# Attention of a hybrid diffusion block: high and low part of a head's queries stacked in the 128 rows, and values of two units at one visit

## What is computed

```python
def attend_with_sink(q, k, v, sink, mask):
    s = jnp.einsum("bqhgd,bkhd->bhgqk", q, k, preferred_element_type=jnp.float32) * (HEAD_DIM ** -0.5)
    if mask is not None:
        s = jnp.where(mask, s, NEG_INF)
    sk = sink.astype(jnp.float32)[None, :, :, None, None]
    m = jnp.maximum(jnp.max(s, axis=-1, keepdims=True), sk)
    p = jnp.exp(s - m)
    denom = jnp.sum(p, axis=-1, keepdims=True) + jnp.exp(sk - m)
    return jnp.einsum("bhgqk,bkhd->bqhgd", (p / denom).astype(v.dtype), v)
```

## Time and profile before

| | |
|---|---|
| three runs | 1251.46, 1252.09, 1252.34 us (median 1252.09) |
| the profiled execution | 1252.31 us, of which the span of instructions is 1250.5 us |
| TensorE busy | 1241.1 us (99%) |
| VectorE, ScalarE, GpSimd busy | 913.3, 560.5, 340.7 us (73%, 45%, 27%) |
| granted TensorE clock | 0.999 over the span |
| mean DMA rate | 160 GB/s |

### The profile page before, as it was taken

The page is one execution under the profiler, slowest core; times in us unless marked ns, Lnnn a source line. Parts: engine busy times, 40 slices in busy tenths (PEclk is TensorE's granted clock), DMA queues, the critical chain, the costliest instruction groups (busy, mean ns, idle before and its releaser), DMA issues.

```text
span 1250.5 us, 19713 instructions
## 1 busy us (share of the span) xinstructions
PE 1241.1 (99%) x7504; PEld 1074.4 (86%) x7504; DVE 913.3 (73%) x1229; ACT 560.5 (45%) x912; POOL 340.7 (27%) x270
## 2 busy tenths in 40 slices
PE   8999999999999999999999999999999999999998
PEld 6788777787888898888888888899999999998996
DVE  4799889562898777662879674577897566778677
ACT  5223465653423345332223332344676645754554
POOL 1006699110143001111001110003693130144243
PEclk9999999999999999999999999999999999999999
DMA  9666422112466416562555664335433554556553
GB/s 380 221 214 197 147 65 71 65 54 99 143 191 227 136 61 203 186 225 80 182 166 188 212 194 145 122 119 189 150 123 118 175 178 138 186 185 207 180 170 116
DMA packets 52804, 200.33 MB, mean 160 GB/s; under 512 B 6001, under 2 KB 7921, under 8 KB 51569
## 3 DMA queue, kind: packets, MB, share of 16 engines
q1 hardware_dynamic: 52576, 199.13, 48.5%
q10 hardware_dynamic: 144, 0.07, 0.0%
HBM read 196.81 MB, written 1.05 MB: 158 GB/s over the span
## 4 chain that ended last, share of the span: by engine, by line
PE 97%; DVE 1%; ACT 0%; DMA 0%; issue 0%; DVEq 0%
PE psA L640 25%; PE psA L642 25%; PE psA L641 25%; PE psB L642 3%; PE psB L640 3%; PE psB L641 3%; PE psB L993 2%; PE psB L981 2%; PE psB L1140 2%; PE psB L1141 2%; PE psB L1142 2%; PE psA L968 1%; PE psA L646 1%; PE psA L651 1%; PE psA L647 1%; PE psB L675 1%
## 5 line engine op out<-in xcount | busy, mean ns | idle before, releaser
L640 PE MATMUL psA<-h_hi,w_hi 128*128 128x512 f32 (+1 forms) x1448 | 491.5, 339 | 0.1
L642 PE MATMUL psA<-h_hi,w_lo 128*128 128x512 f32 (+1 forms) x1448 | 488.0, 337 | 0.0
L641 PE MATMUL psA<-h_lo,w_hi 128*128 128x512 f32 (+1 forms) x1448 | 487.9, 337 | 0.0
L1196 ACT ACTIVATE w_hi<-raw 128x1024 fp32r<-128x1024 f32 (+2 forms) x246 | 274.2, 1117 | 278.0 <-PE psA L642 166.8
L1565 DVE TENSOR_TENSOR w_lo<-raw,w_hi 128x1024 fp32r<-128x1024 f32 (+2 forms) x246 | 339.4, 1380 | 61.5 <-ACT w_hi L1196 61.0
L640 PEld LDWEIGHTS psA<-h_hi,w_hi 128*128 128x128 f32 x1448 | 274.8, 190 | 29.9 <-DVE w_lo L1565 0.9
L642 PEld LDWEIGHTS psA<-h_hi,w_lo 128*128 128x128 f32 x1448 | 274.8, 190 | 29.1
L641 PEld LDWEIGHTS psA<-h_lo,w_hi 128*128 128x128 f32 x1448 | 274.9, 190 | 28.5 <-issue 0.2
L627 POOL TENSOR_TENSOR hid_lo<-sig,hid_hi 128x512 f32 (+3 forms) x44 | 68.6, 1558 | 441.5 <-ACT hid_hi L1513 441.5
L1597 DVE SCALAR_TENSOR_TENSOR ada_sum<-raw,csil,ada_sum 128x1024 f32<-128x1024 f32 x112 | 156.7, 1430 | 0.0
L2058 DVE SCALAR_TENSOR_TENSOR tmp<-psA,vec,tmp 128x510 f32<-128x510 f32 (+1 forms) x44 | 27.1, 615 | 68.3 <-ACT tmp L1524 68.1
(11 more groups left out here) (246 smaller groups left out, 1814.2 us busy)
## 6 DMA issues: line engine op xcount, KB each, us to landing
raw<-w_up SPq DMA_DIRECT2D x88, 512.0 KB, 4.3
raw<-w_ada SPq DMA_DIRECT2D x80, 512.0 KB, 3.5
raw<-w_in SPq DMA_DIRECT2D x35, 512.0 KB, 4.3
raw<-w_at SPq DMA_DIRECT2D x24, 512.0 KB, 3.5
raw<-w_dn SPq DMA_DIRECT2D x16, 704.0 KB, 5.2
raw<-w_dn SPq DMA_DIRECT2D x22, 512.0 KB, 3.5
raw<-w_fn SPq DMA_DIRECT2D x16, 640.0 KB, 4.1
raw<-w_sc SPq DMA_DIRECT2D x16, 640.0 KB, 3.9
```

The costliest lines, as they stand in the source:

```text
L640: pe.matmul(out, w0, hi, start=first, stop=False)
L641: pe.matmul(out, w0, lo, start=False, stop=False)
L642: return pe.matmul(out, w1, hi, start=False, stop=last)
L1196: act.activation(w_hi[:, s, 0:tiles * P], raw[:, r, 0:tiles * P], ACT.Copy).then_inc(head_done, 1)
```

## The change

Scores. The split queries of a head now lie above each other: `q_two[:, b, half, :]` holds for one head the high part in the 64 partitions of its own half and the low part in the other 64. `k_two[half]` holds the high part of that half's keys twice, in both sets of 64 partitions. One matmul over 128 rows then gives high times high plus low times high. The product with `k_lo` remains a 64-row matmul for each half. The mask band comes after the stacked matmuls.

ScalarE therefore makes four copies of 64 by 512 keys instead of one of 128 by 512, and two copies of 64 by 128 queries per unit instead of one of 128 by 128. VectorE makes the low keys and the low queries in two instructions each; the low queries are written into the partitions of the other half. ScalarE's key copies wait for one more semaphore (`evac`, an event of the stage before), since `k_two[1]` lies in memory that the stage before used.

Values. `values` does nothing for even units and does two units at an odd one: the transposed weights of two units stand side by side (in the first layer in unused ends of the weight slots, `prob_tails`; in the second in unused columns of `h_hi` and `h_lo`, `prob_pair`), and one matmul takes 256 columns. In the first layer the first two key blocks belong to the latent unit alone and stay at 128 columns. `y_hi` and `y_lo` are made for two units at once.

```diff
-        q_hi = place("q_hi", [2, P], F32R)
-        q_lo = place("q_lo", [2, P], F32R)
+        q_two = place("q_two", [2, 2, P], F32R)
...
-        k_hi = at("k_hi", [NT], F32R, sqa_off)
+        k_two = [at("k_two0", [NT], F32R, sqa_off), at("k_two1", [NT], F32R, t_off + 4 * NT * 2)]
...
-                    pe.wait_ge(q_rest, b0 + k + 1)
+                    pe.wait_ge(q_rest, 2 * (b0 + k + 1))
                     b = (b0 + k) % 2
+                    for half in range(2):
+                        pe.matmul(score_bank(layer, half)[:, 0:nk * P], q_two[:, b, half, :],
+                                  k_two[half][:, k0 * P:(k0 + nk) * P], start=True, stop=False, skip_group_check=True)
                     if s == 0:
                         for half in range(2):
                             pe.matmul(score_bank(layer, half)[:, (1 - qi) * P:(2 - qi) * P], band[:, 2, :],
-                                      band[:, qi, :], start=True, stop=False, skip_group_check=True)
-                    for part, (qs, ks) in enumerate(((q_hi, k_hi), (q_hi, k_lo), (q_lo, k_hi))):
-                        for half in range(2):
-                            rows = slice(64 * half, 64 * half + 64)
-                            mm = pe.matmul(score_bank(layer, half)[:, 0:nk * P], qs[rows, b, :],
-                                           ks[rows, k0 * P:(k0 + nk) * P], start=(s == 1 and part == 0),
-                                           stop=(part == 2), skip_group_check=(s == 0))
...
+                                      band[:, qi, :], start=False, stop=False, skip_group_check=True)
+                    for half in range(2):
+                        rows = slice(64 * half, 64 * half + 64)
+                        pe.matmul(score_bank(layer, half)[:, 0:nk * P], q_two[rows, b, half, :],
+                                  k_lo[rows, k0 * P:(k0 + nk) * P], start=False, stop=True, skip_group_check=True)\
+                            .then_inc(s_mm, 1)
...
                 def values(k):
-                    s, qi, t = un[k]
-                    k0, nk = (0, 4) if s == 0 else (2, 2)
+
+                    if k % 2 == 0:
+                        return
                     pe.wait_ge(pt, 2 * (b0 + k) + 2)
-                    if b0 + k:
-                        pe.wait_ge(o_rest, b0 + k)
-                    for b in range(nk):
+                    if b0 + k > 1:
+                        pe.wait_ge(o_rest, b0 + k - 1)
+                    for b in range(4):
+                        n = P if layer == 0 and b < 2 else 2 * P
...
+                            mm = pe.matmul(out_bank[64 * half:64 * half + 64, 0:n],
+                                           v[:, b, 64 * half:64 * half + 64],
+                                           prob, start=(b == 0), stop=(b == 3),
+                                           skip_group_check=True)
+                    mm.then_inc(o_mm, 2)
...
-                    act.activation(q_hi[:, (b0 + k) % 2, :], q[:, t, q0:q0 + P], ACT.Copy).then_inc(q_head, 1)
+                    for half in range(2):
+                        rows = slice(64 * half, 64 * half + 64)
+                        act.activation(q_two[rows, (b0 + k) % 2, half, :], q[rows, t, q0:q0 + P], ACT.Copy).then_inc(q_head, 1)
 
                 act.wait_ge(rope, 15 * (layer + 1))
-                act.activation(k_hi[:, :], k_all[:, :], ACT.Copy).then_inc(k_head, 1)
+                act.wait_ge(evac, n0 + 16)
+                for half in range(2):
+                    for into in range(2):
+                        act.activation(k_two[half][64 * into:64 * into + 64, :], k_all[64 * half:64 * half + 64, :], ACT.Copy)\
+                            .then_inc(k_head, 1)
...
+                    for half in range(2):
+                        rows, others = slice(64 * half, 64 * half + 64), slice(64 - 64 * half, 128 - 64 * half)
+                        dve.tensor_tensor(q_two[others, (b0 + k) % 2, half, :], q[rows, t, q0:q0 + P],
+                                          q_two[rows, (b0 + k) % 2, half, :].bitcast(F32), ALU.subtract).then_inc(q_rest, 1)
+
+                dve.wait_ge(k_head, 4 * (layer + 1))
+                for half in range(2):
+                    rows = slice(64 * half, 64 * half + 64)
+                    dve.tensor_tensor(k_lo[rows, :], k_all[rows, :], k_two[half][rows, :].bitcast(F32), ALU.subtract)\
+                        .then_inc(k_rest, 1)
```

More of the change, by code:

```diff
@@ L440, in wide, with two_units @@
             return (4 if batches(layer)[k][0] == 0 else 2) * P
+        def two_units(layer, y, unit):
+            _, qi, t = unit
+            if layer:
+                return y[:, 3 + t:5 + t, P * qi:P * qi + P]
+            return y[:, 4 + t, :].rearrange("p (s n) -> p s n", s=2)[:, :, P * qi:P * qi + P]
         block = ctx.enter_context(nc.Block())
@@ L952, in scores @@
                     if k == 0:
-                        pe.wait_ge(k_rest, layer + 1)
+                        pe.wait_ge(k_rest, 2 * (layer + 1))
                         pe.wait_ge(v_done, layer + 1)
@@ L1854, in query_rest @@
                     q0 = SEQ * s + P * qi
[L1855 to L1860 removed]
+                    dve.wait_ge(q_head, 2 * (b0 + k + 1))
+                    for half in range(2):
[7 more added lines that the diff above has]
+                        .then_inc(k_rest, 1)
                 for k in range(2):
```

52 lines of the change are left out of this document (27 added, 25 removed).

## The result

| | before | after |
|---|---|---|
| median | 1252.21 us (1251.46 to 1253.94, 6 runs) | 1260.03 us (1259.02 to 1261.73, 6 runs) |
| profiled execution, span | 1252.31, 1250.5 us | 1259.02, 1257.2 us |

The ratio is 1.0063, 95% interval 1.0052 to 1.0073: slower, by 7.8 us. The forecast was 1253.0, range 1250.2 to 1255.8.

The account below looks back on a forecast made before the run. TensorE's streaming plus mode switches was taken to bound the kernel, any new TensorE wait adding in full. Terms -1.7 + 1.9 + 0.2 + 0.3 + 0.2 = +0.9 us gave a median of 1253.0, range 1250.2 to 1255.8.

Parts of the forecast that it names:

- Scores, 0: TensorE's score matmuls: three times 0.23 us per unit before and after, mode switches alike; 0, bounds -2.4 to +2.4 us.
- Values, -1.7: TensorE's values: same columns, but 24 visits become 12, each saving 0.14 us; -1.7 us, bounds 0 to -2.5.
- Transposes earlier, +0.2 and +0.3: Second layer, places 4 and 12: TensorE reaches odd units' transposes earlier and waits for ScalarE's shares; +0.2 and +0.3 us.
- Start of the second layer, +1.9: Second layer's attention start: TensorE's first scores wait for four key copies, then VectorE's low keys and low queries; +1.9 us.
- fifth rival: Behind 884 us: a 2 to 3 us wait drops TensorE's clock to 1.2 GHz, costing about 3 more; 1256 us, chance 0.04.
- Low queries in the first layer, +0.2: VectorE, first layer: the second low-query subtraction follows the first without waiting for GpSimd, costing 0.2; +0.2 us, bounds 0 to 5.
- second rival: VectorE's second subtractions each lose the shared port lock to GpSimd, 0.5 to 1.0 us: 1255.4 to 1258 us, chance 0.25.

Follow-up runs that it names:

- old_helpers: Kernel after's stacked score matmuls, but one key copy, one query copy and one subtraction each as before, values as before; output differs: 1252.94 us against 1252.39.
- values_only: Kernel before with only the values part of the change (two units per visit), six score matmuls and old helpers kept: 1251.41 us against 1252.34.
- small_taps_after: Kernel after with GpSimd's taps 1 to 30 working on 2 columns per stream instead of 256: 1253.40 us, ratio 1.0003 to before.
- three_pairs: The change's scores part alone with all its helper work, but TensorE takes scores as three half-row pairs; output differs: 1261.19 us, ratio 1.0066.
- all_in_two: Kernel before with ScalarE's key and query copies, low-query and low-key subtractions all in pieces of 64 partitions: +7.9 us, ratio 1.0060.
- again_low: Kernel before with an unread 64-partition, 64-column subtraction from partition 0 behind each low-query subtraction, no added signal: 1252.39 us against 1252.35.

## Why the prediction was wrong

**Scores, 0: right.** old_helpers is +0.3 us in the first layer and 0.0 at the second start, within 0.2%.

**Values, -1.7 (0.14 a visit): right.** The first layer of values_only is -1.2 for 8 visits, 0.14 each. In the second layer, from 888.5 to 975 us, it loses 0.5 with a wait of 1.27 in it, so about 0.8 is saved for four visits.

**Transposes earlier, +0.2 and +0.3: wrong in size, and without effect.** In values_only it is 0 at place 4 and 1.27 at place 12, outside my bound of 0.8. In the kernel after there is no wait at either place; I take it that this is because TensorE comes 4.6 us later there.

**Start of the second layer, +1.9: too small; measured 4.6.** I had 1.3 us of wait without GpSimd and 1.9 with it; measured are 2.06 and 2.87. Of the 0.7 that is missing without GpSimd, 0.4 are the copies, whose distance for 64 partitions is 0.65 and not the 0.52 that I took, and 0.3 the subtractions, which start 0.72, 0.72 and 0.32 apart in small_taps_after where I had 0.63, 0.63 and 0.20. The lock adds 0.8. The other 1.7 us come behind the wait: in the table of differences the kernel after loses 3.1 us up to the first branch matmul and 1.5 over the next 3.6 us, where the clock is at 1.2 GHz for the most part. That was my fifth rival, with 0.04; I had its price as 3.

**Low queries in the first layer, +0.2: the step that failed.** It says that the second subtraction follows the first, by the row at 194.03. That row is one of 128 partitions from partition 0, like the one ahead of it; it says nothing of the new ones, which alternate between partitions 0 and 64 and each signal. VectorE and GpSimd in the kernel after, against the earlier trace rows:

```profile
177.11 1.95 DVE L1887 TENSOR_TENSOR q_two<-q,q_two 64x128 fp32r<-64x128 f32 x2
178.98 1.27 DVE L1918 TENSOR_REDUCE small<-psA 128x1 f32<-128x512 f32 x2
...
176.84 1.28 POOL L598 TENSOR_TENSOR acc<-acc,sqb 128x512 f32<-128x512 f32 x1
178.22 0.70 POOL L596 TENSOR_SCALAR sqb<-glu,vec 128x512 f32<-128x512 f32 x1
```

The first waits for the end of L598 (178.12) and the second for that of L596 (178.92); in the earlier trace rows one took 1.29 in all. The term was 0.2 and 4.6 + 1.2 = 5.8 was lost there; 5 was my bound. TensorE's waits in that layer add up to 4.8 (0.4, 1.44, 0.36, 1.09 and 1.45); the trace has no wait for the other 1.0. The second rival had the mechanism and for "1.0 per unit" a first layer of 4 to 5 and 1258 us: that is what happened, with the clock on top. The Trainium skill's rule in "SBUF — State Buffer", section "SBUF: two separate sides", which I cited against the change, is borne out: the second one of a pair lasts 0.53 to 1.36 us in 23 of the 24 pairs of the kernel after and 0.29 in one. I gave that rival 0.25 because one row seemed to speak against it.

**Open.** three_pairs loses 1.1 us more in the first layer than all_in_two. The difference between them in VectorE is that the low queries go to the partitions of the other half, and ScalarE puts the transposed weights into other memory; the intervals of the two times overlap, and it was not taken apart further.

## What to carry to other kernels

A row tells the cost of another instruction only if it has the same start partition and signals as well as the same size, and if the other engine comes at the same moment: look at the distance of two starts against the end of the first before using a row as proof that an instruction "follows at once". Small delays do not simply add up: three of 1.1, 1.3 and 0.6 us gave 7.9 together. They shared one cover, and their waits together brought TensorE's clock down. Price a new wait of TensorE with the slower stretch behind it.

## What the hardware showed unexpectedly

- A second low-query subtraction starts 0.08 us ahead of the end of the first if both start at the same partition. If not, it starts 0.014 us after the end, or 0.031 if the first signals. Where GpSimd's tap was issued 0.05 us ahead of that end, it went first in the last case alone, and 64 by 64 elements took 0.68 us instead of 0.21. Issued 0.12 us ahead, it went first in spite of the overlap (1.34 us at 229.42 in again_low).
- ScalarE shows the same kind of gap: four copies of 64 partitions by 512 take 2.58 us, 0.65 from one to the next, where one of 128 partitions lets the next start after 0.52.
- Behind waits of 2.0, 2.06, 2.87 and 2.9 us at the same place TensorE's granted clock went to 0.50 for some microseconds; behind 0.54 and 1.2 there, and behind the 1.09 to 1.45 of the first layer, it stayed at 1.00. The wait of 2.06 cost 3.7 us in all and that of 2.87 cost 4.6.
